# Gated recurrence in a two-block layer stack: decays kept as running products in q and k, a new order of stages in mixer 0, and a barred bank in mixer 1

## What is computed

```python
f = lb[l] + (1.0 - lb[l]) * jax.nn.sigmoid(f_raw)
q = jax.nn.silu(q_raw)                       # k = 1 - f, v = i_raw, 6 heads of 128
# S_t = diag(f_t) S_{t-1} + k_t v_t^T, o_t = S_t^T q_t, chunkwise
diff = c_[:, :, :, None, :] - c_[:, :, None, :, :]          # c_ = cumsum(log f)
decay = jnp.exp(jnp.where(tri[:, :, None], diff, -jnp.inf))
scores = jnp.einsum('bhtd,bhsd,bhtsd->bhts', q_, k_, decay)
o = einsum('bhts,bhsv->bhtv', scores, v_) + einsum('bhtd,bhdv->bhtv', q_ * exp(c_), state)
state = exp(c_end)[..., None] * state + einsum('bhsd,bhsv->bhdv', k_ * exp(c_end - c_), v_)
main = merge_heads(rms_norm(o, hgrn_o_gain[l])) * jax.nn.silu(g_raw)
```

## Time and profile before

| | |
|---|---|
| runs | 1742.43, 1743.12, 1744.99 us; median 1743.12 us |
| profiled execution | 1740.66 us, of which the span is 1738.8 us |
| mean granted clock of TensorE | 0.979 |
| TensorE busy | 1650.6 us (95%) |
| DVE, ACT, POOL busy | 1047.5, 872.0, 98.1 us |
| mixer 0 of the second block | about 794 to 960 us of the span |

### The profile page before, as it was taken

The page is one execution under the profiler, slowest core; times in us unless marked ns, Lnnn a source line. Parts: engine busy times, 40 slices in busy tenths (PEclk is TensorE's granted clock), DMA queues, the critical chain, the costliest instruction groups (busy, mean ns, idle before and its releaser), DMA issues.

```text
span 1738.8 us, 27205 instructions
## 1 busy us (share of the span) xinstructions
PE 1650.6 (95%) x11578; PEld 1523.2 (88%) x11578; DVE 1047.5 (60%) x1506; ACT 872.0 (50%) x1297; POOL 98.1 (6%) x72
## 2 busy tenths in 40 slices
PE   7999999999999899999789999999999998789999
PEld 7989887998977799999778899989999997679998
DVE  6875565886655655556785645555546455555554
ACT  5975464685455445346445533344453456444332
POOL 0112000012100000000330000000000000000000
PEclk9999999999999899999999999998999999899999
DMA  6624234543314565555321555544655553035552
GB/s 223 196 69 134 72 95 126 174 142 110 96 55 136 167 212 177 192 178 165 119 73 52 191 189 180 188 132 136 211 186 186 181 168 112 25 122 182 183 193 97
DMA packets 204298, 253.24 MB, mean 146 GB/s; under 512 B 17809, under 2 KB 183953, under 8 KB 204049
## 3 DMA queue, kind: packets, MB, share of 16 engines
q1 hardware_dynamic: 204176, 251.49, 45.4%
HBM read 250.43 MB, written 1.05 MB: 145 GB/s over the span
## 4 chain that ended last, share of the span: by engine, by line
PE 79%; DVE 8%; ACT 6%; issue 5%; DMA 1%; POOL 1%; SPq 0%; DVEq 0%; ACTq 0%; POOLq 0%
PE bank L788 77%; ACT arena L1395 4%; DVE weights_rest L1913 2%; DVE arena L2060 1%; PE bank L846 1%; ACT weights_high L1395 1%; ACT L1390 1%; DMA ring<-in_w_in 1%; ACT L1395 0%; DVE small L2232 0%; DVE x L2278 0%; PE bank L1165 0%; DVE weights_rest_more L1913 0%; DVE arena L2250 0%; POOL arena L2546 0%
## 5 line engine op out<-in xcount | busy, mean ns | idle before, releaser
L788 PE MATMUL bank<-xT_high,weights_high 128*128 128x256 f32 (+1 forms) x2352 | 673.3, 287 | 7.4 <-DVE xT_rest L2006 3.1
L788 PE MATMUL bank<-xT_rest,weights_high 128*128 128x256 f32 (+1 forms) x2352 | 656.8, 283 | 0.0
L788 PE MATMUL bank<-xT_high,weights_rest 128*128 128x256 f32 (+1 forms) x2048 | 579.3, 284 | 0.0
L1913 DVE TENSOR_TENSOR weights_rest<-ring,weights_high 128x1024 fp32r<-128x1024 f32 (+3 forms) x414 | 486.6, 1224 | 97.1 <-ACT weights_high L1395 93.3
L1395 ACT ACTIVATE weights_high<-ring 128x1024 fp32r<-128x1024 f32 (+3 forms) x414 | 400.5, 1019 | 252.5 <-PE bank L788 235.7
L788 PEld LDWEIGHTS bank<-xT_high,weights_high 128*128 128x128 f32 (+1 forms) x2352 | 452.4, 192 | 18.0 <-issue 7.9
L788 PEld LDWEIGHTS bank<-xT_rest,weights_high 128*128 128x128 f32 (+1 forms) x2352 | 446.7, 192 | 2.9 <-issue 1.7
L788 PEld LDWEIGHTS bank<-xT_high,weights_rest 128*128 128x128 f32 (+1 forms) x2048 | 393.7, 192 | 0.5
L1395 ACT ACTIVATE arena<-bank 128x512 f32<-128x512 f32 (+4 forms) x253 | 133.9, 547 | 375.2 <-PE bank L788 321.2
L788 PE MATMUL bank<-arena 128*128 128x128 f32 (+3 forms) x1416 | 202.3, 302 | 30.2 <-ACT arena L1395 17.0
L788 PEld LDWEIGHTS bank<-arena 128*128 128x128 f32 (+1 forms) x1416 | 175.6, 200 | 55.4 <-issue 24.4
(11 more groups left out here) (180 smaller groups left out, 1700.5 us busy)
## 6 DMA issues: line engine op xcount, KB each, us to landing
ring<-in_w_in SPq DMA_DIRECT2D x36, 1024.0 KB, 5.3
ring<-in_ffn_w_gate SPq DMA_DIRECT2D x36, 1024.0 KB, 5.3
ring<-in_ffn_w_up SPq DMA_DIRECT2D x35, 1024.0 KB, 5.4
ring<-in_ffn_w_down SPq DMA_DIRECT2D x34, 1024.0 KB, 4.9
ring<-in_w_out SPq DMA_DIRECT2D x22, 1024.0 KB, 4.9
ring<-in_w_in_a SPq DMA_DIRECT2D x11, 1024.0 KB, 5.2
ring_more<-in_ffn_w_down SPq DMA_DIRECT2D x10, 1024.0 KB, 4.9
ring_more<-in_ffn_w_up SPq DMA_DIRECT2D x9, 1024.0 KB, 5.4
```

The lines of the kernel that those rows point to most:

```text
L788: return eng.matmul(o, a, b, start=first, stop=last)
L1913: TTs(rest_slot(b)[:, part], raw_slot(b)[:, part], high_slot(key)[:, part].bitcast(F32), ALU.subtract).then_inc(*dv.mark(("rest", key, z)))
```

## The change

The logarithm, its cumulated sums and the exponentials go. `spans` keeps running products of f over blocks of 2, 4 and so on up to 64 tokens, made once in `hg_f`. `hX` starts as q times f (`hg_q`, now on DVE), and `hk` as 1 - f. After each level DVE multiplies the right halves of q by the product of the left block and the left halves of k by the product of the right block, in place (`carry`). What the last level leaves in `hX` and `hk` is what the state and the second chunk's output need, so `hg_kd` goes and `hg_kdT` transposes `hk` itself. The level's matmuls take `hk` and `hX` as two operands. POOL has no part in the levels any more. The Silu of the gate is taken for the first four heads in one piece and for the last two in the copy out of the bank.

The order of stages: the gate's projections 1 and 2 and the state come behind level 64, and both score steps of the memory attention stand at level 16. The order in which the weights are used is as before. In `st_pv` of TensorE the two transpose groups of `("pv", "m0", 0)` and `("pv", "m1", 0)` may take any bank but the one of `("o", l, 0)`.

```diff
-            out += [("pa", "q", 1), ("pa", "q", 2), ("hg_q",), ("hg_diff", 1), ("pa", "i", 0), ("hg_d",)]
-            fill = {1: [], 2: [("pa", "i", 1), ("hg_kd",)], 4: [("pa", "qm", 0)], 8: [("pa", "i", 2), ("memq", l)],
-                    16: [("pa", "g", 0), ("hg_state",), ("att", "e0", 0)], 32: [("sm", "e0", 0), ("pa", "g", 1), ("att", "e0", 1)],
-                    64: [("pv", "e0", 0), ("sm", "e0", 1), ("pa", "g", 2), ("hg_g",)]}
+            out += [("pa", "q", 1), ("pa", "q", 2), ("hg_q",), ("pa", "i", 0), ("hg_d",)]
+            fill = {1: [], 2: [("pa", "i", 1)], 4: [("pa", "qm", 0)], 8: [("memq", l), ("pa", "i", 2)], 16: [("att", "e0", 0), ("att", "e0", 1)],
+                    32: [("sm", "e0", 0), ("sm", "e0", 1), ("pa", "g", 0)], 64: [("pv", "e0", 0)]}
             for s in LEVELS:
-                out += fill[s] + ([("hg_diff", 2 * s)] if 2 * s in LEVELS else []) + [("hg_level", s)]
+                out += fill[s] + [("hg_level", s)]
+            out += [("pa", "g", 1), ("hg_g",), ("hg_kdT",), ("pa", "g", 2), ("hg_state",)]
...
+                held = new.bank[("o", int(name[1]), 0)] if (name[0], hp) == ("m", 0) else None
                 for t in range(NT):
                     nk = kw(name, t) // P
                     pe.wait_ge(*at(("p", name, hp, t)))
-                    b = group(("pt", name, hp, t))
+                    b = group(("pt", name, hp, t), among=None if held is None else [i for i in range(8) if i != held])
...
+            def st_hg_kdT(st):
+                pe.wait_ge(*at(("hX", P)))
...
-                        ins = eng.transpose(b[:, h * P:h * P + P], kd[:, a + h, :], ident)
+                        ins = eng.transpose(b[:, h * P:h * P + P], hk[:, a + h, 0:P], ident)
...
-                        X = hX[:, h, n * P:n * P + P]
-                        ins = mm(b[:, i * P:i * P + P], X, X)
+                        ins = mm(b[:, i * P:i * P + P], hk[:, h, n * P:n * P + P], hX[:, h, n * P:n * P + P])
...
-                    copy(mix2[:, two, :], st, v, ("gate", kind, j), func=ACT.Copy if kind == "pa" else ACT.Sigmoid)
+                    copy(mix2[:, two, :], st, v, ("gate", kind, j), func=ACT.Sigmoid if kind == "pb" else ACT.Silu if j == 2 else ACT.Copy)
...
-                A(hc, hE, ACT.Ln).then_inc(*ac.mark(("hlf",)))
...
                 A(qf, qf, ACT.Silu).then_inc(*ac.mark(("hq",)))
-                load_table(ACT.Exp)
...
-                A(mix2[:, 0:6, :], mix2[:, 0:6, :], ACT.Silu).then_inc(*ac.mark(("gates",)))
-                load_table(ACT.Exp)
...
+                A(mix2[:, 0:4, :], mix2[:, 0:4, :], ACT.Silu).then_inc(*ac.mark(("gates",)))
...
-                A(hE, hE, ACT.Exp).then_inc(*ac.mark(("hEe", s)))
...
-                for h in range(H_H):
-                    eng.tensor_tensor_scan(hc[:, h, :], C("restart"), hc[:, h, :], 0.0, ALU.mult, ALU.add).then_inc(*dv.mark(("hc",)))
...
+                for s in LEVELS[:-1]:
+                    a, b = totals(s)
+                    dv.wait_ge(*dv.last())
+                    TTs(span(2 * s), a, b, ALU.mult).then_inc(*dv.mark(("spans", 2 * s)))
+
+            def span(s):
+
+                at_ = 6 * S - 12 * S // s
+                return hE.rearrange("p a b -> p (a b)") if s == 1 else spans[:, at_:at_ + 6 * S // s]
+
+            def totals(s):
+
+                v = span(s).rearrange("p (n z) -> p n z", z=2)
+                return v[:, :, 0], v[:, :, 1]
+
+            def st_hg_q(st):
                 dv.wait_ge(*at(("hq",)))
+                TTs(hX, qf, hE, ALU.mult).then_inc(*dv.mark(("hX", 1)))
+
+            def carry(s):
+
+                left, right = totals(s)
+                (kl, _), (_, qr_) = halves(hk, s), halves(hX, s)
+                if s < LEVELS[-1]:
+                    TTs(qr_, qr_, bcast(left, s), ALU.mult).then_inc(*dv.mark())
+                    TTs(kl, kl, bcast(right, s), ALU.mult).then_inc(*dv.mark(("hX", 2 * s)))
+                    return
...
-                TTs(er, cr, ref, ALU.subtract).then_inc(*dv.mark())
-                TTs(el, ref, cl, ALU.subtract).then_inc(*dv.mark(("hE", s)))
...
             def st_hg_level(st):
                 s = st[1]
+                dv.wait_ge(*at(("hl", s, 2)))
+                dv.wait_ge(*at(("hX", s)))
+                dv.wait_ge(*at(("spans", LEVELS[-1])))
+                carry(s)
...
-                    T(xx[:, :, 1, :], q[:, :, 1, :], e[:, :, 1, :], ALU.mult).then_inc(*po.mark())
-                    T(xx[:, :, 0, :], k[:, :, 0, :], e[:, :, 0, :], ALU.mult).then_inc(*po.mark(("hX", s)))
```

More of the change, by code:

```diff
@@ L529, in two_blocks @@
         qf = view(6, S)
-        hc = view(6, S)
+        spans = view(6 * S)
         hk = view(6, S)
@@ L1336, in st_hg_o @@
                     pe.wait_ge(*at(("hSs", g)))
-                    pe.wait_ge(*at(("qe",)))
+                    pe.wait_ge(*at(("hX", P)))
                     for h in range(m):
@@ L1801, in st_px @@
                     copy(kf[:, two, :], st, v, (kind, "k", "raw", j))
-            def st_hg_f(st):
-                ac.wait_ge(*at(("hf",)))
-                A(hc, hE, ACT.Ln).then_inc(*ac.mark(("hlf",)))
-                ac.wait_ge(*ac.last())
             def st_hg_q(st):
@@ L1812, in st_hg_q, with st_hg_kdT @@
                 A(qf, qf, ACT.Silu).then_inc(*ac.mark(("hq",)))
-                load_table(ACT.Exp)
             def st_hg_g(st):
-                for j in range(3):
+                for j in range(2):
                     ac.wait_ge(*at(("gate", "pa", j)))
-                A(mix2[:, 0:6, :], mix2[:, 0:6, :], ACT.Silu).then_inc(*ac.mark(("gates",)))
-                load_table(ACT.Exp)
-            def st_hg_kd(st):
-                ac.wait_ge(*at(("kdd",)))
-                A(kd, kd, ACT.Exp).then_inc(*ac.mark(("kde",)))
-                ac.wait_ge(*ac.last())
-                A(qe, hc[:, :, P:S], ACT.Exp).then_inc(*ac.mark(("qee",)))
+                A(mix2[:, 0:4, :], mix2[:, 0:4, :], ACT.Silu).then_inc(*ac.mark(("gates",)))
+            def st_hg_kdT(st):
+                for g, (a, n) in enumerate(((0, 4), (4, 2))):
+                    copy(kdT[:, a:a + n, :], ("kdT", g), ps(("kdT", g), n, P), ("kdTs", g))
             def st_hg_state(st):
                 for g, (a, n) in enumerate(((0, 4), (4, 2))):
-                    copy(kdT[:, a:a + n, :], ("kdT", g), ps(("kdT", g), n, P), ("kdTs", g))
-                for g, (a, n) in enumerate(((0, 4), (4, 2))):
                     copy(hS[:, a:a + n, :], ("hS", g), ps(("hS", g), n, P), ("hSs", g))
-            def st_hg_diff(st):
-                s = st[1]
-                ac.wait_ge(*at(("hE", s)))
-                A(hE, hE, ACT.Exp).then_inc(*ac.mark(("hEe", s)))
             def st_hg_o(st):
@@ L1885, in _ @@
                      memkn=st_memkn, memq=st_memq, pa=st_px, pb=st_px, pk=st_px,
-                     memke=st_memke, hg_q=st_hg_q, hg_kd=st_hg_kd, hg_g=st_hg_g, hg_d=None,
-                     hg_f=st_hg_f, hg_state=st_hg_state, hg_level=None, hg_o=st_hg_o, fox_q=st_fox_norm,
+                     memke=st_memke, hg_q=st_hg_q, hg_kdT=st_hg_kdT, hg_g=st_hg_g, hg_d=None,
+                     hg_f=None, hg_state=st_hg_state, hg_level=None, hg_o=st_hg_o, fox_q=st_fox_norm,
                      fox_k=st_fox_norm, fox_s=st_fox_s, fox_d=st_fox_d, fox_e=st_fox_e)
@@ L2442, in st_hg_n @@
                     dv.wait_ge(*at(("gates",)))
+                    dv.wait_ge(*at(("gate", "pa", 2)))
                     r = rn2[:, g, :, :].rearrange("p a b -> p (a b)")[:, 0:m * P].rearrange("p (a b) -> p a b", a=m)
@@ L2460, in _ @@
                      norm=st_norm, ab=st_ab, abt=st_abt, parts=st_parts, hg_n=st_hg_n, proj=st_proj, lru=st_lru, decay=st_decay, l2=st_l2, mla_norm=st_mla_norm,
-                     gdn_a=st_gdn_a, tri=None, trid=st_trid, gdn_u=None, gdn_w=st_gdn_w, gdn_n=st_gdn_n, sc=None, gdn_o=None, uq=st_uq, rot=st_rot, ukv=st_ukv, att=st_att, sm=st_sm, hg_diff=st_hg_diff, pv=st_pv,
+                     gdn_a=st_gdn_a, tri=None, trid=st_trid, gdn_u=None, gdn_w=st_gdn_w, gdn_n=st_gdn_n, sc=None, gdn_o=None, uq=st_uq, rot=st_rot, ukv=st_ukv, att=st_att, sm=st_sm, pv=st_pv,
                      outp=st_outp, final=st_final, ffn=st_ffn, norm_front=st_norm_front, norm_part=st_norm_back, memkv=st_memkv,
                      norm_turn=None, norm_in=st_norm_back, memkn=st_memkn, memq=st_memq, pa=st_px, pb=st_px, pk=st_px,
-                     memke=None, hg_q=None, hg_kd=st_hg_kd, hg_g=None, hg_d=st_hg_d,
+                     memke=None, hg_q=st_hg_q, hg_kdT=None, hg_g=None, hg_d=st_hg_d,
                      hg_f=st_hg_f, hg_state=None, hg_level=st_hg_level, hg_o=None, fox_q=st_fox_norm,
```

46 lines of the change are left out of this document (10 added, 36 removed).

## The result

The changed kernel took 1724.73 us (median of four runs, 1723.91 to 1726.08), the kernel before 1742.78 in the same set (1740.85 to 1744.99): ratio 0.9893, 95% interval 0.9878 to 0.9908. It is faster by 18 us; 1724.5 was forecast. The profiled execution took 1724.89 us, its span is 1722.8. Profile against profile, 18.7 us were forecast and 15.8 came (1740.66 less 1724.89).

A forecast was written before the change was run, and what follows sets the result against it. TensorE, busy 95% of the span, was the bound. 24.6 us of idle and slow time, less 4.65 waits, 1.6 clock and 1.3 table, plus 1.6 in mixer 1, gave 18.7 us: median 1724.5, range 1718 to 1733.

The forecast's parts named there:

- The bound: Whole kernel: TensorE, busy for 95% of the span; an edit gains only from its idle time or lower-clock time.
- Start: Start of the recurrence: six products take 2.6 us, the split wait shrinks from 2.1 to 0.65, level 1 doesn't wait.
- A level: Levels of mixer 0's recurrence: carry ready at +1.8 us against +5.8, so four waits go; level 16 is just hidden.
- Level 64: Last level of the recurrence: DVE's chain of 19.5 us comes late, a new TensorE wait of 3.3 us.
- The slow time that the old kernel has in the stretch: Old recurrence in mixer 0: lower-clock time behind three long waits, 5.2 us in all, that the change could win.
- The clock at level 64: Behind the new wait at the last level: full clock taken as lost, costing 1.6 us; ends 0 and 2.2.
- Mixer 1: First block, both layers: pv inherits the bank wait, gdn_o 1 starts at full clock; 0.8 us a layer, 1.6 together.
- The step from the profiled time to the median: Whole kernel: the median lies 2.5 us above the profiled execution, taking 1722.0 to 1724.5 us.
- 1 (DVE late at every level): Recurrence levels: matmuls wait 1.8 us each at five levels, 9 us, about 1733.5 us; chance 0.18.
- 2 (carries cost as on POOL): Carries: each as slow as POOL's products; gain gone at 2.8 us each, or about 2.3 with half clock; chance 0.07.
- 3 (the bank does nothing): Mixer 1: pv inherits the wait and DVE holds gdn_o 1 anyway; 1.6 us less gain, 1726 us; chance 0.15.
- 4 (clock kept at level 64): Last level: clock kept and DVE's queue drains faster; 3 to 4 us more gain, 1721 us; chance 0.2.

The follow-up runs named there:

- e9: Changed kernel with two extra products on DVE before each carry of levels 2 to 32, into an unread buffer; 1729.83 us, 0.9929 of the kernel before.
- e6: Changed kernel with the carries of all seven levels moved from DVE to POOL; 1728.08 us, 0.9914 of the kernel before.
- e7: Changed kernel with DVE's split of g1's weights and second softmax put behind level 32's carries and copies; 1723.47 us, 0.9891 of the kernel before.
- e10: Changed kernel measured again with nothing edited; 1727.34 us, 0.9913 of the kernel before.
- e1: Kernel before with only the barred bank for mixer 1's transpose groups added; 1741.11 us, 0.9981 of the kernel before.
- e11: Changed kernel with mixer 1's bank barred for the first attention product (pv) too, not only its transposes; 1723.93 us, 0.9893 of the kernel before.
- e2: Changed kernel without the barred bank; 1725.51 us, 0.9888 of the kernel before.
- e3: Changed kernel's recurrence with the gate's projections and memory attention left in their old places; 1725.38 us, 0.9884 of the kernel before.
- e4: Old recurrence (logarithms, exponentials, POOL's products) in the new order of stages, with the barred bank; 1755.50 us, 1.0057 of the kernel before.
- e5: Changed kernel with ACT loading the exponential table ahead of the squares of hg_o 0; 1722.16 us, 0.9884 of the kernel before.
- e12: Changed kernel with early exponential table, DVE's work ahead of level 64 put off, and mixer 1's bank barred for pv; 1716.80 us, 0.9831 of the kernel before.

## Why the prediction was right, point by point

**The bound** was right: e9's added work on DVE cost only where TensorE had to wait for it, and in the slow time behind such waits.

**Start.** Six products took 2.69 us against 2.6, and the split wait is 0.72 against 0.65. `hX` came at 837.25, with the stretch 1.18 us later than before, so 836.07 against 836.0. Level 1 doesn't wait.

**A level.** The carries take 0.96 and 0.95 us, `hX` 1.76, the copies as before. No wait at levels 1 to 32, as forecast. Groups of DVE by form in mixer 0, answering to the earlier trace rows:

```profile
L1898 DVE TENSOR_TENSOR weights_rest<-ring,weights_high 128x1024 fp32r<-128x1024 f32 x29 | 34.1, 1219 | 18.7 <-ACT weights_high L1396 18.6
...
L2397 DVE TENSOR_TENSOR arena<-arena 128x768 f32<-128x768 f32 x6 | 5.7, 950 | 0.0
```

The splits are back at 1.22 us from 1627 ns, as the prediction read from a split with POOL idle. In e6, with POOL busy again, their mean is 1356 ns.

**Level 64.** DVE's chain took 19.1 us (869.26 to 888.35) against 19.5, and the wait 2.65 against 3.3. e7 and e9 show that it is this chain. With 3.8 us taken out the wait goes. With the products that e9 adds at levels 8, 16 and 32, 5.2 us, the chain is 24.3 us long (867.92 to 892.18), TensorE itself comes 3.4 us later by its wait at level 16 and the slow time behind it, and the wait grows by 1.8.

**Terms that were off.** (1) The slow time that the old kernel has in the stretch: I had 5.2 us, it is 6.3 (the busy time of the windows). I measured two losses by the stretched instructions of one level each and the loss behind 912 from its 4-us window, and missed what lies beside. (2) The clock at level 64: 1.6 us taken as lost. It was kept in the first profile and lost in the second. (3) The wait there, 0.65 us too long. Together 3.4 us of the 3.7 by which the stretch's 20.8 exceeds the forecast 17.05; in e10, with two losses in the stretch, it is 17.5. (4) Mixer 1: I had 1.6 us from gdn_o 1 starting at full clock. The rows give 1.1 in e1, whose median is 3.3 lower (1.6 to 4.9), and 0.4 in the changed kernel's own profile, where both layers lost the clock. The mechanism (pv inherits the bank, the subtraction holds gdn_o 1) is shown by e11; that the clock is then kept was the weak part. (5) Nothing was set aside for the clock outside the stretch. There the changed kernel's profile is 4.8 us longer, where 1.6 less was forecast. (6) The step from the profiled time to the median, 2.5 us, came out as -0.2. So the stretch gave 3.7 us more than forecast, the rest of the kernel 6.4 less, and the step 2.7 less to add: that these cancel to 0.2 us is luck, and the recurrence's 20.8 against 17.05 is the fair measure of the prediction.

**Rivals.** 1 (DVE late at every level): even double carries are late at two places only. 2 (carries cost as on POOL) by the 0.95-us rows. e6, with the carries on POOL itself, is still faster than before; its products took 1.9 us in the mean, below the 2.3 to 2.8 that the rival needs to eat up the gain. 3 (the bank does nothing) holds for the places of the work; e1's median speaks against it under the old recurrence, and under the new one (e2) it is neither shown nor refuted. 4 (clock kept at level 64) is what the first profile shows, and what e10 takes back.

## What to carry to other kernels

Where an engine chain feeds TensorE step by step, compare the chain's length per step with the TensorE work that can stand beside it. When it is shorter than the cover, its exact cost and the places of the cover matter little (e3, e6); when it is longer, a move of the cover alone costs 0.6% (e4). Before explaining a difference between two profiles, split each stretch into TensorE's idle and busy time: idle time came out the same to 0.1 us in two executions of one kernel, while busy time moved by over 3 us. A lower busy time is not yet a shorter stretch, though: in e11 the idle time took most of it back. When work moves to another queue, list what already waits in that queue (memq in e6), and after mending a late split look at the next one (g2 in e7).

## What the hardware showed that I had not expected

The clock's losses have sizes. The fourteen traces hold 207 stretches at the lower level, leaving out the one at each trace's end; counted as half their length, 147 cost 1.7 us, 34 cost 3.4, 24 cost 5.1 and 2 cost 6.8, and less where TensorE idled in them. Some also come and go behind the same wait: at level 64 waits of 2.65 to 2.68 us were followed by full clock in four profiles (the changed kernel, e2, e5, e11) and by 1.2 GHz in one (e10), which is the changed kernel again; ahead of the first output product 2.84 us kept the clock in three profiles (the changed kernel, e3, e6) and lost it in four (e2, e7, e9, e10). The work ahead of the stretch, the same in all but a few banks, kept TensorE busy for 755.9 (e11) to 766.2 us (e10) and took 793.1 (e12) to 798.0 us (e10). A reader of one profile should take some 5 us as open for this alone.

One and the same product of 768 columns took 1.49 to 3.18 us on POOL in e6, and 0.94 to 0.96 us each time on DVE. DVE was busy for 5.27 of the 5.30 us of the longest carry (844.80 to 850.10), but also for 2.85 of 3 beside a short one (884.5 to 887.5), so that it is busy doesn't explain it. What it does there makes the difference. DVE in e6 beside the one and the other:

```profile
845.57 5.64 DVE L1898 TENSOR_TENSOR weights_rest<-ring,weights_high 128x1024 fp32r<-128x1024 f32 x2
884.51 2.33 DVE L2422 COPY_PREDICATED arena<-const,bank 128x512 f32<-128x512 uint32 x3
```

The two longest products, 3.18 and 2.85 us, run wholly beside a pair of weight splits, and the splits, 2.35 us a pair elsewhere, take 5.64 and 4.96 there. Beside the predicated copies neither is longer: the copies take 2.33 us and the products 1.53 each.
